# Hybrid decoder, two layers: FFN weights as the moving operand, residual stream token by token, adaLN sums moved into the attention

## The reference, cut to what matters

```python
mod = (cond @ ada_w[l] + ada_b[l]).reshape(bsz, 9, 1, dm)
u = rms_norm(h, norm_g[l, 0]) * (1.0 + sc1) + sh1
h = h + 0.5 * g1 * swiglu(u, ffn_w_in[l, 0], ffn_w_out[l, 0])
u = rms_norm(h, norm_g[l, 1]) * (1.0 + sc2) + sh2
h = h + g2 * hybrid_mixer(u, ..., w_in[l], w_out[l], ...)
u = rms_norm(h, norm_g[l, 2]) * (1.0 + sc3) + sh3
h = h + 0.5 * g3 * swiglu(u, ffn_w_in[l, 1], ffn_w_out[l, 1])
```

## Time and profile before

| | us |
|---|---|
| median of 3 runs | 1290.47 (1287.22 to 1290.71) |
| the profiled execution | 1293.87 |
| its span | 1292.1 |

### The profile page before, as it was taken

The page is one execution under the profiler, slowest core; times in us unless marked ns, Lnnn a source line. Parts: engine busy times, 40 slices in busy tenths (PEclk is TensorE's granted clock), DMA queues, the critical chain, the costliest instruction groups (busy, mean ns, idle before and its releaser), DMA issues.

```text
span 1292.1 us, 20135 instructions
## 1 busy us (share of the span) xinstructions
PE 1219.8 (94%) x8511; PEld 1068.1 (83%) x8511; DVE 881.5 (68%) x1609; ACT 437.6 (34%) x713; POOL 18.7 (1%) x30
## 2 busy tenths in 40 slices
PE   3699999998989999999999999999898999999998
PEld 3699999856456689999989999995545767999998
DVE  5878776577875576777568777648595666665553
ACT  2333333211154443333233333321113444333332
POOL 5000000000000000000000000000000000000000
PEclk9999999897969989999999999999796998999999
DMA  9898875197003348777648988626900241766630
GB/s 352 312 317 301 300 266 203 42 282 239 0 1 131 115 150 290 268 269 249 199 157 293 302 312 298 224 67 231 258 32 1 74 142 64 244 204 207 210 131 33
DMA packets 150925, 250.96 MB, mean 194 GB/s; under 512 B 8102, under 2 KB 126516, under 8 KB 142644
## 3 DMA queue, kind: packets, MB, share of 16 engines
q1 hardware_dynamic: 150132, 248.38, 56.9%
q10 hardware_dynamic: 704, 1.30, 0.3%
HBM read 248.62 MB, written 1.05 MB: 193 GB/s over the span
## 4 chain that ended last, share of the span: by engine, by line
PE 80%; DVE 12%; DMA 4%; ACT 1%; issue 1%; SPq 1%; DVEq 0%; ACTq 0%
PE ps L516 38%; PE ps L543 8%; PE ps L544 7%; PE ps L545 7%; DMA ada<-in_ada_w_dram 4%; PE ps L606 4%; PE ps L647 2%; PE ps L488 2%; PE ps L626 2%; PE ps L635 2%; PE ps L625 1%; PE ps L481 1%; DVE acc L1227 1%; DVE sq L1186 1%; PE ps L648 1%
## 5 line engine op out<-in xcount | busy, mean ns | idle before, releaser
L1255 DVE TENSOR_TENSOR wl<-wide,wh 128x2048 fp32r<-128x2048 f32 x88 | 201.4, 2290 | 16.3 <-ACT wh L874 16.3
L543 PE MATMUL ps<-fh,th 128*128 128x256 f32 x704 | 200.4, 285 | 0.9 <-DVE fl L1310 0.9
L899 ACT ACTIVATE fs<-ps 128x256 f32<-128x256 f32 x88 | 33.7, 383 | 489.9 <-PE ps L516 472.3
L545 PE MATMUL ps<-fh,tl 128*128 128x256 f32 x704 | 199.1, 283 | 0.0
L544 PE MATMUL ps<-fl,th 128*128 128x256 f32 x704 | 199.1, 283 | 0.0
L516 PE MATMUL ps<-uh,wh 128*128 128x256 f32 x1344 | 189.0, 283 | 2.0 <-DVE wl L1255 2.0
L516 PE MATMUL ps<-ul,wh 128*128 128x256 f32 x1344 | 188.7, 283 | 0.0
L516 PE MATMUL ps<-uh,wl 128*128 128x256 f32 x1344 | 188.7, 283 | 0.0
L516 PEld LDWEIGHTS ps<-uh,wh 128*128 128x128 f32 x1344 | 173.3, 192 | 2.6 <-DVE wl L1255 2.6
L516 PEld LDWEIGHTS ps<-ul,wh 128*128 128x128 f32 x1344 | 173.4, 192 | 0.0
L516 PEld LDWEIGHTS ps<-uh,wl 128*128 128x128 f32 x1344 | 173.4, 192 | 0.0
(11 more groups left out here) (256 smaller groups left out, 1382.7 us busy)
## 6 DMA issues: line engine op xcount, KB each, us to landing
wide<-in_ffn_w_in_dram SPq DMA_DIRECT2D x88, 1024.0 KB, 8.2
ada<-in_ada_w_dram SPq DMA_DIRECT2D x60, 1024.0 KB, 5.6
tall<-in_ffn_w_out_dram SPq DMA_DIRECT2D x44, 1024.0 KB, 4.9
wide<-in_w_in_dram SPq DMA_DIRECT2D x14, 1024.0 KB, 8.1
tall<-in_w_out_dram SPq DMA_DIRECT2D x8, 1024.0 KB, 7.9
ada<-in_ada_w_dram SPq DMA_DIRECT2D x16, 512.0 KB, 8.3
wide<-in_c_cmp_w_dram SPq DMA_DIRECT2D x4, 1024.0 KB, 17.2
wide<-in_w_in_dram SPq DMA_DIRECT2D x4, 832.0 KB, 6.0
```

Source lines behind the costliest of these rows:

```text
L543: mm(y[:, d, :], th[:, a, cols], hi, start=False, stop=False, skip_group_check=True)
L545: i = mm(y[:, d, :], tl[:, a, cols], hi, start=False, stop=False, skip_group_check=True)
L899: A(fs[:, m % 2, :], ps[:, m % 2, 0:SEQ], ACT.Silu).then_inc(silu_ready, 1)
L1255: tt(wl[:, a, :, :, :].rearrange("p e k n -> p (e k) n"), raw, wh[:, a, :, :, :].rearrange("p e k n -> p (e k) n").bitcast(F32), ALU.subtr ...
```

## The change

**Operands swapped.** `h` is kept as `h[128, 2, 1024]`: 128 tokens of a half by 1024 features. In `gate_up` the stationary operand is `uh` or `ul` (128 features x 128 tokens), the moving one 2 x 256 weight columns, gate and up of a whole pair; a block b of 256 hidden columns takes 8 (k) x 2 (token halves) x 3 = 48 matmuls of 512 columns. In `add_rows` the hidden values are stationary and 512 columns of `w_out` move: 24 per block. The hidden block is token by token after that, so four f32 transposes per block (`turn_f`) precede `down`, and ScalarE and VectorE split it from PSUM.

**Low halves in place.** `wlo` and `tlo` lie over `wide` and `tall`. A half of a `wide` slot is refilled when the matmuls of that half are done (`gu_ready`), `tall` when `down` is done (`down_done`). A `wide` fill is four DMAs.

**Norm.** ScalarE's squares sum along the free dimension (`accum_out`); VectorE scales rows (`scale_rows`), TensorE turns them (`turn_rows`, 16 transposes), VectorE applies scale and shift from PSUM (`modulate`), ScalarE rounds. No matmul takes part in the statistics.

**Gates** lie along the free dimension, so they are summed by f32 matmuls of 512 columns with `ones`, and added to `ada_b` rows broadcast by a DMA (`grow`). Shifts and scales are summed by 16 one-column matmuls (`sums`).

**The mixer's sums** move into the attention: `ada_sum` in steps 4, 6 to 18, their loads behind the mixer's other loads, `sums` in step 21. The first block's weights of the second FFN are split in steps 12 to 19.

**The output** is stored from `h`, in four DMAs, without transposes.

The diff, cut to its core:

```diff
-ADA_ROUNDS = (8, 6)
+ROUNDS = (5, 3)
+MIX_ADA = {4 + 2 * k: k for k in range(KD)}
+MIX_SUM = NJ - 3
+PRE_HI = {12 + 2 * c: c for c in range(4)}
+PRE_LO = {13 + 2 * c: c for c in range(4)}
...
+        wlo = nc.alloc_sbuf_tensor_at("wlo", [P, 2, 2, KD, 2 * P], F32R, offset=WIDE0)
...
+        tlo = nc.alloc_sbuf_tensor_at("tlo", [P, 2, 2, DM], F32R, offset=TALL0)
...
+            def ffn_wide(l, f, b, c):
+
+                n = (WIDE_A, WIDE_B)[f] + b
+                if b >= 2:
+                    sp.wait_ge(gu_ready, gu_at(l, f, b - 2, c))
...
+                for b in range(NB):
+                    for c in range(2):
+                        if b + 2 < NB:
+                            ffn_wide(l, f, b + 2, c)
+                        if b < KD:
+                            ada_piece(l, f, b, c)
+                    if b + 1 < NB:
+                        ffn_tall(l, f, b + 1)
...
+            def gate_up(l, f, b):
...
                 for k in range(KD):
...
                     for t in range(NT):
...
+                        o = ps[:, gu_bank(b, t), :].rearrange("p (e n) -> p e n", e=2)
+                        rows_ = slice(t * P, (t + 1) * P)
+                        mm(o, uh[:, k, rows_], wh[:, hsl, :, k, :], start=(k == 0), stop=False, skip_group_check=True)
+                        mm(o, ul[:, k, rows_], wh[:, hsl, :, k, :], start=False, stop=False, skip_group_check=True)
+                        i = mm(o, uh[:, k, rows_], wlo[:, s, :, k, :], start=False, stop=(k == KD - 1),
+                               skip_group_check=True)
...
+            def turn_f(l, f, b):
+
                 for t in range(NT):
...
+                    pe.wait_ge(fa_s, ff_at(l, f, b, t, 2))
+                    for a in range(2):
+                        i = tr(ps[:, 2, a * SEQ + t * P:a * SEQ + (t + 1) * P], fa[:, t, a * P:(a + 1) * P], ident)
+                i.then_inc(ft_ready, 1)
...
+            def mod_round(l, f, r):
...
+                pe.wait_ge(mod_red, rounds_at(l, f, r) - 1)
+                if r == 2:
+                    i = sums(acc, ps[:, 3, :], DM)
+                else:
+                    col = (r if r < 2 else 3 + r) * 512
+                    i = mm(ps[:, 3, :], ones[:, :], acc[:, col:col + 512], start=True, stop=True)
...
+                gate_up_first(l, f)
+                for b in range(1, NB):
+                    gate_up(l, f, b)
+                    if b in (1, NB - 1):
+                        down(l, f, b - 1, ((0, 0), (0, 1)))
+                        turn_f(l, f, b)
+                        down(l, f, b - 1, ((1, 0), (1, 1)))
+                    else:
+                        down(l, f, b - 1)
+                        turn_f(l, f, b)
+                    for r in {NB - 3: (0, 1), NB - 2: (2, 3), NB - 1: (4,)}.get(b, ()):
+                        if r < rounds:
+                            mod_round(l, f, r)
+                down(l, f, NB - 1)
...
+                for b in range(NB):
+                    if b:
+                        rest_f(l, f, b - 1)
+                    for c in range(4):
+                        if b + 1 < NB:
+                            rest_wide(l, f, b + 1, c)
...
+                    if 1 <= b <= KD:
+                        ada_step(l, f, b - 1, 1)
...
+                    for a in range(2):
+                        rest_tall(l, j, 2 * b + a)
+                    for t in range(NT):
+                        dve.wait_ge(silu_ready, ff_at(l, f, b, t, 2))
+                        tt(fa[:, t, :], fs[:, t, :], ps[:, gu_bank(b, t), SEQ:2 * SEQ], ALU.mult).then_inc(fa_s, 1)
+                    if b < KD:
+                        ada_step(l, f, b, 0)
```

More of the change, by code:

```diff
@@ L448, in layer @@
                           (proj, projected(l, F_CMPIN)))
-                for k in range(6, KD):
-                    ada_mix(l, k)
                 n += 1
@@ L539, in add_rows @@
-            def add_rows(a, hi, lo, last, done=None, tiles=range(KD)):
-                for d in tiles:
-                    cols = slice(d * P, (d + 1) * P)
-                    mm(y[:, d, :], th[:, a, cols], hi, start=False, stop=False, skip_group_check=True)
-                    mm(y[:, d, :], th[:, a, cols], lo, start=False, stop=False, skip_group_check=True)
-                    i = mm(y[:, d, :], tl[:, a, cols], hi, start=False, stop=False, skip_group_check=True)
-                    if last and d % 2:
-                        i.then_inc(y_ready, 1)
-                    elif done is not None and d == KD - 1:
-                        i.then_inc(done, 1)
@@ new lines, in down @@
+            def down(l, f, b, parts=((0, 0), (0, 1), (1, 0), (1, 1))):
+                if parts[0] == (0, 0):
+                    pe.wait_ge(tl_ready, rows_at(l, 2 * f, 2 * b + 1))
+                    pe.wait_ge(mul_ready, ff_at(l, f, b))
+                if b == 0 and parts[0] == (1, 0):
+                    pe.wait_ge(fa_s, ff_at(l, f, 1, 1, 2))
+                add_rows(((TALL_A, TALL_B)[f] + b) % 2, [(fh[b % 2][:, a, :], fl[b % 2][:, a, :]) for a in range(2)], range(2),
+                         b == 0, b == NB - 1, down_done if parts[-1] == (1, 1) else None, parts)
@@ L567, in sum_parts @@
                 i.then_inc(mod_ps, 1)
             def ffn(l, f, last=False):
+                rounds = ROUNDS[f] - last
                 if l or f:
-                    norm_stats(l, 2 * f)
-                open_y()
+                    keep_warm(16)
+                    turn_rows(l, 2 * f)
                 gate_up_first(l, f)
-                for i in range(KD // 2):
-                    for q in range(4):
-                        gate_up(l, f, q + 1, i)
-                        down(l, f, q, i)
@@ L1361, in ffn @@
-                dve.wait_ge(gate_ready, 3 * l + (2 if f == 0 else 3))
-                residual(l, j)
-                if last:
-                    return
+                    scale_rows(l, j)
+                else:
+                    for c in range(4):
+                        rest_wide(l, f, 0, c)
+                modulate(l, j, uf, range(4))
+                for k in range(KD):
+                    dve.wait_ge(u_ready, u_at(l, j, k))
+                    tt(ul[:, k, :], uf[:, k, :], uh[:, k, :].bitcast(F32), ALU.subtract).then_inc(ul_ready, 1)
@@ L1387, in mixer @@
             def mixer(l):
[L1388 to L1394 removed]
+                scale_rows(l, 1)
+                modulate(l, 1, u, (0, 2))
                 dve.wait_ge(s_small, (l + 1) * 160)
[L1396 removed]
                 copied(l, 0)
```

684 lines of the change are left out of this document (326 added, 358 removed).

## The result

The changed kernel took 1335.51 us (median of 4 runs, 1329.75 to 1338.90), the kernel before 1290.59 beside it: ratio 1.035, 95% interval 1.030 to 1.039. It is slower; forecast were 1247, a range from 1225 to 1288, and 0.82 for faster. The profiled execution has a span of 1337.1 us at a mean granted clock of 0.937 (before 1292.1 at 0.959). Since the granted clock has two levels here, 1.00 (2.4 GHz) and 0.50 (1.2 GHz), that is (1 - 0.937) x 2 x 1337 = 168 us at 1.2 GHz against 106. The record of the clock begins only at 49 us in the one profile and at 42 in the other, so low clock in the prologue before that is in neither figure.

A forecast was written before the change was run, and what follows sets the result against it. TensorE was taken as the bound, its 256-column FFN matmuls paced at 0.120 us by weight loads. The terms, led by -76.0 us for the pitch, summed to -43.4, giving 1247 us from 1290.5; range 1225 to 1288.

The forecast's parts named there:

- The pitch: FFN matmuls: 0.216 us per 512 columns in place of 0.120 per 256, a gain of 76.0 us.
- Rival 2: Every fp32r matmul, long or short, carries the 13 ns: pitch 0.227, +36 us, 1283 us; chance 0.12.
- Rival 1: In all 3360 new matmuls the stream is the limit: pitch 0.240, +81 us, 1328 us; chance 0.10.
- The attention: VectorE's added products and subtractions, `sums` and fewer matmuls: +8.2 us in each attention, twice +16.4.
- The start of the blocks: Start of each FFN: TensorE waits for late loads and `fa`, +21.0 us, and low clock behind three waits, +4.8.
- The four first tiles of before: In the four FFNs of the old kernel, the first tile's waits for VectorE go away: -8.8 us.
- Rounds of the modulation: FFN modulation sums: 512-column matmuls (0.86 us each), one-column sums (3.5 us a set) and waits for VectorE, together +17.0 us.
- The mixer's middle: Eight `ada_sum`, load waits and transposes leave it, so the attention starts 12.1 us earlier, twice: -24.2 us.
- Between the stages: From the last FFN matmul to the next stage 8.5 us, 10.5 after the attention; sum -3.3 us.
- End: The output loses transposes and copies: 4.6 us for 10.2, -5.6 us.
- Prologue: Less waiting by VectorE before the first matmul, which comes at 45.4 us for 49.3: -3.9 us.
- The signs that the prediction set for itself: A matmul pitch over 0.229 us, or blocks of over 17.3 us, would prove the forecast wrong.

The follow-up runs named there:

- experiment 1: Changed kernel with nine series of 64 matmuls appended, differing in type, columns, stationary tile and bank: 1434.46 us (one run).
- experiment 4: Changed kernel with seven of the mixer's modulation products a layer left out of the attention on VectorE: 1312.82 us, ratio 1.017 to the kernel before.
- experiment 5: Changed kernel with each set of 16 one-column modulation sums replaced by one matmul of 16 columns: 1311.39 us, ratio 1.018 to the kernel before.
- experiment 10: One-column sums spread out instead of in one run: on experiment 9's kernel 1269.89 us, alone on the changed kernel 1329.65 us.
- experiment 11: As `e10_four`, but the attention's sums in another bank, eight behind step 25's values and eight behind step 26's: 1276.19 us, ratio 0.989 to the kernel before.
- experiment 6: Changed kernel with the mixer's eight products and the subtractions of `wlo` moved to other attention steps: 1315.30 us, ratio 1.020 to the kernel before.
- experiment 2: Changed kernel with the load of `tall` of block 1 issued ahead of block 2's wide loads and modulation rows: 1333.97 us, ratio 1.033 to the kernel before.
- experiment 7: Experiment 2 plus the modulation's rows one block later, on the changed kernel: 1320.09 us, ratio 1.025 to the kernel before.
- experiment 9: Changed kernel with experiments 6 and 7 and a layer's ten small loads issued behind its first fills: 1296.27 us, ratio 1.003 to the kernel before.
- e10_four: Experiment 9's kernel with the one-column sums spread over the last `gate_up` and attention steps 23 to 25: 1269.89 us, ratio 0.983 to the kernel before.
- experiment 8: Changed kernel with the mixer's products on GpSimd instead of VectorE, from attention step 2 on: 1422.72 us, ratio 1.104 to the kernel before.

## Why the prediction was wrong

- **The pitch: wrong, and the largest single term.** The step that failed is "213.3 + 2.5 = 0.216", taken from the plain f32 rows. Rival 2, "The 13 ns above 107 belong to each fp32r matmul", is what holds; its chance of 0.12 was too low. The argument against it, "at the low clock they are not seen", is true of the rows, here too (0.426), and proves nothing: the 13.3 ns show at 2.4 GHz only. The price is 3360 x 0.0107 = 36 us (experiment 1). The reading of the earlier trace rows, a load of 0.12 us that explains the old pitch, was an accident of 256 columns, whose 106.7 + 13.3 ns make the same 0.120; with 128 columns, where the load could show, it is 0.111. Rival 1 (0.240) is out.
- **The attention: sign right, size wrong**, +45.0 for +16.4. VectorE's work and its lateness were foreseen. That the lateness and the run of sums turn into 34.1 and 20.5 us at half clock was not: the sum has no term for it. Experiments 4, 5, 10 and 11 show that either of them takes the clock down and that both have to go (with the reserve on the sums' place). "`sums` in step 21 costs TensorE 3.5" was 6.98, since the clock was down already; where it was not, the sums brought it down (experiment 6).
- **The start of the blocks: waits right**, 21.1 for 21.0 us, with their cause as told in part only: not `tall` alone but all that lies ahead of `fa` (experiments 2 and 7). The low clock behind them was 6.8, 3.4, 6.8 and 3.4 us, at most 10 us of time for the forecast 4.8. (The four first tiles of before, 1.6, 1.6, 3.9 and 1.6, make 8.7 and not 8.8.)
- **Rounds of the modulation**: the 0.87 and 3.5 hold, but the clock falls in or behind the sums: 3.4, 3.4 and 6.8 us low, 6.8 us of time with no term in the forecast. The kernel before had a sign of it: each norm's 32 one-column matmuls stand between its stages, and behind four of the five that begin at full clock the profile has 3.4 to 6.8 us of low clock (246.9, 458.5, 871.5, 1083.1). The change took these out, which is part of the better time between the stages, and put others inside the stages.
- **The last block of layer 0**: 3.1 us and a low stretch of 3.4, not foreseen. SyncE's order was not followed from one layer into the next.
- **Feed-forward together**: 53 us over the forecast, of which 33.9 are the pitch, 3.1 the boundary and at most 14 the low clock beyond the forecast 4.8. About 2 us are not placed.
- **The mixer's middle**: right, -21.7 for -24.2. **Between the stages**: better than forecast, 7.3 to 7.7 us for 8.5 (10.7 and 10.9 after the attention); the forecast's own terms give -2.5 and not -3.3, and before it was 50.3 us and not 49.0. **End**: 4.0 for 4.6, but -3.6 for -5.6 since 7.6 of before was put at 10.2 (the last feed-forward matmul starts at 1284.4 and not at 1282). **Prologue**: +1.2 for -3.9; the sums there took 6.98 us instead of 3.5, after 10.7 us of idling. Their pace of 0.218 us is that of the low clock (6.98 us in step 21 too), though this profile has no record of the clock there.
- Pitch 36, attention without its pitch 27, the feed-forward's rest 19, prologue 5 make 87 of the 88 us. With rival 2's pitch alone the forecast would have been 1283, faster by 0.6%. By half the length of its stretches, which is an estimate, the low clock without a term costs 27 us in the attentions and some 14 in the feed-forward. That is nearly the whole loss of 45 us: the longer pitch used up most of the gain, and the clock turned what was left into a loss.
- The signs that the prediction set for itself did not give this away: the pitch stayed under 0.229 and a block under 17.3 us. They watched single matmuls and steady blocks, and the loss was in stretches at half clock between them.

## What to carry to other kernels

Price a matmul from rows of its own type: the fixed part differs by type (13.3 ns for fp32r, 4 for bf16 here) and is hidden at the low clock, so a low stretch can't rule it out. When work moves onto an engine that feeds TensorE, or when matmuls of one column stand in a row, ask what the clock will do: everything behind it then takes up to twice as long, which costs more than the wait itself, and the busy share does not show it. A new load order is checked against the consumer's order of instructions, not only against its own queue.

## What the runs showed of the hardware that was not expected

- fp32r matmuls with a weight load each start 13.3 ns plus their columns at 2.4 GHz apart (0.227, 0.173, 0.120 for 512, 384, 256), and 0.111 us apart for 128; bf16 of 512 columns 0.217 (experiment 1). At 1.2 GHz it is 0.426 for 512, with nothing added.
- The granted clock mostly falls in or right behind a run of 32 one-column f32 passes (3.5 us), with TensorE never idle ahead of it (experiment 6): behind all three of the changed kernel that begin at full clock, all five of experiment 9, and four of five in the kernel before. The one at 661.80 has none behind it, so it is no fixed rule. In the attention the clock then stays at 0.50 for up to 20.5 us of unbroken short matmuls, while the same steps run at 1.00 when it has not fallen before (`e10_four`).
- While GpSimd works on 128 x 2048 elements (5.57 and 4.51 us an operation), a `TENSOR_SCALAR` of VectorE on 128 x 2 elements takes 0.99 us on the mean instead of 0.17; its reductions from PSUM take no longer (experiment 8).
